# The second map's exponentials kept in their PSUM bank, and the mixing weight taken by one VectorE operation with two scalars

## The chip, the cores and the metric

The kernel runs on one core of a Trainium2 chip. The metric is the device time of one execution in microseconds (us), lower is better. The core's engines each run their own queue of instructions and wait for one another by semaphores: PE (TensorE, matmuls), DVE (VectorE), ACT (ScalarE), POOL (GpSimd) and SP (here only a queue of DMAs).

## What is computed

Two layers of a decoder over 512 tokens of width 1024. Each layer is a SwiGLU feed-forward block, a mixer, and a second feed-forward block, each followed by a layer norm. The mixer has three groups of heads; the change touches the differential attention heads:

```python
s = jnp.einsum('bqhmd,bkhmd->bhmqk', q_blk, k) * scale      # m = 0, 1: two maps per head
s = s - slopes[None, :, None, None, None] * dist[None, None, None]
s = jnp.where(dist >= 0, s, NEG_INF)
p = jax.nn.softmax(s, axis=-1)
a = (p[:, :, 0] - lam * p[:, :, 1]).astype(v.dtype)
return jnp.einsum('bhqk,bkhe->bqhe', a, v)
```

With e0 and e1 the exponentials of the two maps and r0 and r1 their row sums, the kernel forms e0 + w e1 with w = -lam r0 / r1, and divides by r0 at the very end.

## The kernel before, in words

All matmuls of size run in fp32 split into a high and a low part (whi, wlo, xhi, xlo), three matmuls for one product. In each layer the attention is one run of 40 steps G = 0 to 39, in five bodies of 8 steps; bodies 1 and 3 (G 8 to 15 and 24 to 31) are the differential heads, two heads of four 128-row query tiles each, so that the width of a step goes 128, 256, 384, 512 and again. There are 32 differential steps in the program. Each step goes through the engines so:

1. PE `scores(G)`: the scores of map m into bank 2*(G%2)+m (L1092, L1094).
2. DVE `row_max(G)`: L1515. Then ACT `exp(G)`: L777, from the bank into s32, with the row sum into rsum. For a differential step there are two, m = 0 and 1.
3. DVE `mix(G)`: L1530 takes the reciprocals of the two row sums, L1532 the weight wlam (one value per partition), L1536 the mix of the two maps, in place in s32.
4. PE `turn_p(G)`: transposes (L1104) into bank 4+G%2; ACT `p_hi(G)` (L784) and DVE `p_lo(G)` (L1542) split it into a high and a low part; PE `values(G)` (L1116, L1118) multiplies by V; DVE `output(G)` (L1553, L1555).

Each engine's order is written out by hand, one G after the other. DVE does per step: row_max(G), output(G-2), mix(G), p_lo(G-1), and then what the body adds (the splits of queries and keys at L1464 and L1469, parts of the output projection's sums at L1283). PE does per step: scores(G), a piece of other matmuls (`between`: projections of later bodies at L1020, in body 3 the early part of the output projection at L857), values(G-2), turn_p(G-1), another piece.

POOL meanwhile loads the stacks of queries and keys of the next body (L574) and takes low parts of weights (L555, a TENSOR_TENSOR over SBUF of 1024 columns), and between its last two stack loads it scales the norm's gain and bias rows (L481, two such operations). The second-to-last stack load waits for the scores of G = 27, the middle of body 3.

The banks 1 and 3 of the second map are used by nothing else in the attention until `turn_y` takes them in body 4.

Of the kernel before, what the change touches and what calls it, by code (L numbers as in the profile page):

```python
# [5 lines left out]
ALU = mybir.AluOpType  # L6
ACT = mybir.ActivationFunctionType
# [14 lines left out]
FOX_P, DIFF_P = FOX_H // 2, DIFF_H // 2  # L22
# [35 lines left out]
STEPS = 2 * NT  # L58
# [29 lines left out]
def build(nc, x_in, a_w, b_w, d_w, gb_row, gb_col, mix_row, mix_col, ws_in, lamv, out):  # L88
    ctx = ExitStack()
    with ctx:  # L90
# [8 lines left out]
        bank = [ctx.enter_context(nc.psum_tensor(f"bank{i}", [P, 512], F32)) for i in range(8)]  # L99
# [10 lines left out]
        s32 = sb("s32", [P, 4, 512])  # L110
# [39 lines left out]
        negm = sb("negm", [P, 4])  # L150
        olo = sb("olo", [P, 2, HD])
        rsum = sb("rsum", [P, 4])
        rinv = sb("rinv", [P, STEPS, 2])
        wlam = sb("wlam", [P, STEPS])
# [6 lines left out]
        nlam1 = sb("nlam1", [P, 1])  # L161
# [86 lines left out]
        exp_ok = [sem(f"exp_ok{m}") for m in range(2)]  # L248
        rinv_ok = sem("rinv_ok")
        wlam_ok = sem("wlam_ok")  # L250
        mixp_ok = sem("mixp_ok")
# [51 lines left out]
        def count(l, G, m):  # L303

            if m == 0:
                return l * ALL + G + 1
            return l * DIFF_P * STEPS + sum(is_diff(g) for g in range(G + 1))
# [322 lines left out]
        def _(act):  # L630
            a = nc.scalar
# [76 lines left out]
            for l in range(L):  # L708
# [60 lines left out]
                def exp(G):  # L769
                    for m in range(2 if is_diff(G) else 1):  # L770
                        act.wait_ge(max_ok[m], count(l, G, m))
                        if G >= 2:

                            act.wait_ge(pt_done, l * ALL + G - 1)
                        w = (G % NT + 1) * P
                        i = 2 * (G % 2) + m
                        a.activation(s32[:, i, 0:w], bank[i][:, 0:w], ACT.Exp, bias=negm[:, i:i + 1],  # L777
                                     accum_out=rsum[:, i:i + 1]).then_inc(exp_ok[m], 1)

                def p_hi(G):  # L780
# [66 lines left out]
        def _(pe):  # L847
# [178 lines left out]
            def turn_y(l, i):  # L1026

                c = (EARLY + LATE)[i][0]
                if i < len(EARLY):
                    b = 6 + i % 2  # L1030
                else:
                    b = 1 + 2 * (i % 2)
                    if i < len(EARLY) + 2:
                        pe.wait_ge(exp_ok[1], (l + 1) * DIFF_P * STEPS)
                if i % len(EARLY) >= 2:

                    pe.wait_ge(yt_ok, l * NC + i - 1)
                if c < FOX_P:
                    pe.wait_ge(o_ok, l * ALL + (PAIRS.index(c) + 1) * STEPS + AHEAD)
                elif c < FOX_P + DIFF_P:  # L1040
                    pe.wait_ge(y_ok, l * DIFF_P + c - FOX_P + 1 + AHEAD)
                for t in range(NT):
                    ins = t_.transpose(bank[b][:, t * P:t * P + P], nat[:, t, c * P:c * P + P], ident[:, :])
                ins.then_inc(yt_done, 1)
# [31 lines left out]
            def heads(l):  # L1076

                def scores(G):
                    b, k = divmod(G, STEPS)
                    hh, t = divmod(k, NT)  # L1080
                    n_ = (t + 1) * P
                    tile = stack[hh]
                    if t == 0:
                        pe.wait_ge(stacked[hh], 32 * (l * BODIES + b + 1))
                    maps = 2 if is_diff(G) else 1
                    for m in range(maps):
                        i = 2 * (G % 2) + m
                        if G >= 2 and count(l, G - 2, m) > 0:

                            pe.wait_ge(exp_ok[m], count(l, G - 2, m))  # L1090
                        for n in (range(2) if maps == 1 else (m,)):
                            t_.matmul(bank[i][:, 0:n_], tile[0:STACK, n, t * P:t * P + P], tile[0:STACK, 2 + n, 0:n_],  # L1092
                                      start=(n == 0 or maps == 2), stop=False)
                        t_.matmul(bank[i][:, t * P:n_], identr[:, :], maskr[:, :], start=False, stop=True).then_inc(s_done[m], 1)  # L1094

                def turn_p(G):
                    if is_diff(G):
                        pe.wait_ge(mixp_ok, count(l, G, 1))
                    else:
                        pe.wait_ge(exp_ok[0], count(l, G, 0))  # L1100

                    pe.wait_ge(o_ok, l * ALL + max(G - 1, 0) + AHEAD)
                    for e in range(G % NT + 1):
                        ins = t_.transpose(bank[4 + G % 2][:, e * P:e * P + P], s32[:, 2 * (G % 2), e * P:e * P + P], ident[:, :])  # L1104
                    ins.then_inc(pt_done, 1)

                def values(G):
                    b, k = divmod(G, STEPS)
                    hh, t = divmod(k, NT)

                    pe.wait_ge(pt_ok, l * ALL + G + 1)
                    vc = PAIRS[b] * 2 * HD + hh * HD

                    both = bank[4 + G % 2][:, 0:2 * HD].rearrange("p (a n) -> p a n", a=2)
                    for e in range(t + 1):
                        t_.matmul(both, pthi[G % 2][:, e * P:e * P + P], vals[:, e, :, vc:vc + HD],  # L1116
                                  start=(e == 0), stop=(e == t), skip_group_check=True)
                        ins = t_.matmul(both[:, 0, :], ptlo[G % 2][:, e * P:e * P + P], vhi[:, e, vc:vc + HD],  # L1118
                                        start=False, stop=(e == t), skip_group_check=True)
                    ins.then_inc(pv_done, 1)  # L1120

                for G in range(ALL):
                    b, k = divmod(G, STEPS)
                    if k == 0 and b <= EARLY_BODY:
                        between = early(l) if b == EARLY_BODY else project(l, b + 2)
                    scores(G)
                    next(between, None)
                    if G >= 2:
                        values(G - 2)
                    if G >= 1:  # L1130
                        turn_p(G - 1)
                    next(between, None)
                    if b == BODIES - 1 and k in LATE_TURNS:
                        turn_y(l, LATE_TURNS[k])
                early_output(l, 6, 2)
                values(ALL - 2)
                early_output(l, 6, 3)
                turn_p(ALL - 1)
                early_output(l, 7, 2)
                early_output(l, 7, 3)  # L1140
                late_weights(l, 0)
                for o in range(2):
                    late_output(l, o, 0)
                values(ALL - 1)
                for o in range(2, 4):
                    late_output(l, o, 0)
                late_weights(l, 1)
                for o in range(2):
                    late_output(l, o, 1)
                turn_y(l, NC - 1)  # L1150
                for o in range(2, 4):
                    late_output(l, o, 1)
                for n in range(2, len(LATE)):
                    late_weights(l, n)
                    for o in range(4):
                        late_output(l, o, n)
                for o in range(4, 8 - HELD):
                    for n in range(len(LATE)):
                        late_output(l, o, n)
# [82 lines left out]
        def _(dve):  # L1242
            v = nc.vector
# [151 lines left out]
            for l in range(L):  # L1395
# [8 lines left out]
                def values(j):  # L1404

                    lo, at, n_ = V_PARTS[j]
                    for t in range(NT):
                        src = bank[t + 4 * (j % 2)]
                        dve.wait_ge(vhi_ok, l * 3 * NT + j * NT + t + 1)
                        if j == 0:  # L1410
# [7 lines left out]
                                       op0=ALU.mult, op1=ALU.min).then_inc(fneg_ok, 1)  # L1418
# [105 lines left out]
                def mix(G):  # L1524

                    i = 2 * (G % 2)
                    j = G % STEPS
                    dve.wait_ge(exp_ok[0], count(l, G, 0))
                    dve.wait_ge(exp_ok[1], count(l, G, 1))
                    v.reciprocal(rinv[:, j, :], rsum[:, i:i + 2]).then_inc(rinv_ok, 1)  # L1530
                    dve.wait_ge(rinv_ok, l * ALL + G + 1)
                    v.scalar_tensor_tensor(out=wlam[:, j:j + 1], in0=rinv[:, j, 1:2], scalar=rsum[:, i:i + 1],  # L1532
                                           in1=nlam1[:, :], op0=ALU.mult, op1=ALU.mult).then_inc(wlam_ok, 1)
                    dve.wait_ge(wlam_ok, count(l, G, 1))
                    w_ = (G % NT + 1) * P
                    v.scalar_tensor_tensor(out=s32[:, i, 0:w_], in0=s32[:, i + 1, 0:w_], scalar=wlam[:, j:j + 1],  # L1536
                                           in1=s32[:, i, 0:w_], op0=ALU.mult, op1=ALU.add).then_inc(mixp_ok, 1)

                def p_lo(G):
# [143 lines left out]
```

## Time and profile before

| | us |
|---|---|
| median of 3 runs | 2052.26 (2048.38 to 2054.08) |
| profiled execution, its own time | 2058.27 |
| its span | 2056.5 |
| PE busy | 1950.1 (95%) |
| DVE busy | 1112.6 (54%) |
| ACT busy | 703.3 (34%) |
| POOL busy | 327.9 (16%) |
| attention of layer 0, about | 488 to 640 in the span |
| attention of layer 1, about | 1500 to 1650 in the span |

The span is the time from the first to the last instruction on the core. An engine's busy time is a sum over stages with different limits, so 95% for PE does not say what a stage waits for: inside the attention that has to be read from the stage itself. PEclk is the clock that TensorE was granted, as a share of 2.4 GHz; 0.50 is 1.2 GHz. DVE, ACT and POOL rows give the duration of an instruction including any time that it was held after its start.

### The profile page before, as it was taken

The numbers are of one execution on the slowest core, as the hardware profiler recorded it, in microseconds if no ns is written. First come the engines' busy times: TensorE is split into PE (matmuls) and PEld (weight loads), VectorE is DVE, ScalarE is ACT, GpSimd is POOL, SyncE is SP. The second block draws the span as 40 slices with busy tenths as digits, with TensorE's granted clock in tenths as the row PEclk, the third lists the DMA queues.
The fourth block names the chain that finished last, engine by engine and source line by source line (L and its number), as shares of the span: only waits on it lengthen the run. The fifth ranks groups of instructions, "written<-read, shape, count | busy, mean of one in ns | idle before, by whom it ended". The sixth has DMA issues, their size and how long they took to land.

```text
span 2056.5 us, 25255 instructions
## 1 busy us (share of the span) xinstructions
PE 1950.1 (95%) x9341; PEld 1632.3 (79%) x9341; DVE 1112.6 (54%) x1792; ACT 703.3 (34%) x1017; POOL 327.9 (16%) x291
## 2 busy tenths in 40 slices
PE   7999999997989999999999999999978899999996
PEld 6888888886777888888788888888867788888885
DVE  6444445562776653444584444546647765444446
ACT  4323322343434433333242222224335343233321
POOL 6000000333314400000150000003332252000002
PEclk9999999998979999999999999999989999999998
DMA  5223233226731323222322223231277132322221
GB/s 219 102 82 107 78 120 110 80 85 176 190 88 62 116 71 119 102 82 102 113 97 88 102 82 120 74 132 70 78 204 193 42 108 78 121 98 86 102 102 41
DMA packets 41922, 216.99 MB, mean 106 GB/s; under 512 B 8724, under 2 KB 9172, under 8 KB 17928
## 3 DMA queue, kind: packets, MB, share of 16 engines
q1 hardware_dynamic: 38984, 200.35, 27.9%
q0 software_dynamic: 2880, 15.90, 3.1%
q8 instruction: 33, 0.54, 0.1%
q14 instruction: 25, 0.20, 0.0%
HBM read 198.28 MB, written 17.93 MB: 105 GB/s over the span
## 4 chain that ended last, share of the span: by engine, by line
PE 80%; DVE 10%; issue 3%; DMA 2%; ACT 2%; SPq 2%; POOL 1%; DVEq 0%; ACTq 0%; POOLq 0%
PE bank L857 74%; PE bank L1020 2%; SPq L391 2%; DVE res L1283 1%; DVE nat L1431 1%; DMA whiD<-stacks 1%; DMA rawA<-in_a_w 1%; PE bank L1116 1%; PE bank L885 1%; DVE st L1307 1%; DVE hl L1358 1%; DVE hl L1542 1%; DVE wlam L1532 1%; PE bank L1104 1%; DVE negm L1515 1%
## 5 line engine op out<-in xcount | busy, mean ns | idle before, releaser
L857 PE MATMUL bank<-whiD,hl 128*128 128x512 f32 x1408 | 444.6, 390 | 5.6 <-DVE hl L1358 5.1
L1283 DVE SCALAR_TENSOR_TENSOR res<-bank,res 128x512 f32<-128x512 f32 x384 | 258.5, 688 | 171.0 <-PE bank L857 168.8
L857 PEld LDWEIGHTS bank<-whiD,hl 128*128 128x128 f32 x1408 | 264.3, 188 | 65.0 <-DVE hl L1358 8.1
L857 PE MATMUL bank<-xhi,whiA 128*128 128x512 f32 (+1 forms) x768 | 287.6, 374 | 10.3 <-DVE xlo L1262 10.3
L857 PE MATMUL bank<-xlo,whiA 128*128 128x512 f32 (+1 forms) x768 | 285.9, 372 | 0.0
L857 PE MATMUL bank<-xhi,wloA 128*128 128x512 f32 (+1 forms) x768 | 285.9, 372 | 0.0
L857 PE MATMUL bank<-wloD,hl 128*128 128x512 f32 x704 | 274.1, 389 | 0.0
L857 PE MATMUL bank<-xhi,whiB 128*128 128x512 f32 x704 | 273.9, 389 | 0.0
L857 PE MATMUL bank<-xlo,whiB 128*128 128x512 f32 x704 | 273.9, 389 | 0.0
L857 PE MATMUL bank<-xhi,wloB 128*128 128x512 f32 x704 | 273.9, 389 | 0.0
L857 PEld LDWEIGHTS bank<-xhi,whiA 128*128 128x128 f32 x768 | 145.5, 189 | 38.0 <-DVE xlo L1262 8.5
L1354 DVE TENSOR_TENSOR s<-s,bank 128x256 f32<-128x256 f32 x88 | 33.1, 418 | 246.7 <-ACT s L690 246.7
L857 PEld LDWEIGHTS bank<-xlo,whiA 128*128 128x128 f32 x768 | 145.5, 189 | 24.9
L857 PEld LDWEIGHTS bank<-xhi,wloA 128*128 128x128 f32 x768 | 145.4, 189 | 25.0
L1251 DVE TENSOR_TENSOR wloA<-rawA,whiA 128x2048 fp32r<-128x2048 f32 x51 | 123.1, 2414 | 74.0 <-ACT whiA L636 74.0
L1347 DVE TENSOR_TENSOR s<-s,bank 128x512 f32<-128x512 f32 x44 | 30.2, 687 | 242.8 <-ACT s L683 242.8
L481 POOL TENSOR_TENSOR gbr<-gbr,alpha 128x1024 f32<-128x1024 f32 x12 | 23.2, 1957 | 862.5 <-DMA gbr<-in_gb_row 862.5
L857 PEld LDWEIGHTS bank<-xhi,wloB 128*128 128x128 f32 x704 | 132.2, 188 | 27.5
L857 PEld LDWEIGHTS bank<-xhi,whiB 128*128 128x128 f32 x704 | 132.2, 188 | 27.3
L857 PEld LDWEIGHTS bank<-xlo,whiB 128*128 128x128 f32 x704 | 132.2, 188 | 27.2
L857 PEld LDWEIGHTS bank<-wloD,hl 128*128 128x128 f32 x704 | 132.2, 188 | 26.9
L690 ACT ACTIVATE s<-bank 128x256 f32<-128x256 f32 x88 | 29.0, 381 | 348.7 <-PE bank L857 348.7
(177 smaller groups left out, 3146.8 us busy)
## 6 DMA issues: line engine op xcount, KB each, us to landing
rawA<-in_a_w SPq DMA_DIRECT2D x63, 1024.0 KB, 4.8
rawB<-in_b_w SPq DMA_DIRECT2D x54, 1024.0 KB, 4.8
rawD<-in_d_w SPq DMA_DIRECT2D x46, 1024.0 KB, 4.8
stacks<-hl SPq DMA_DIRECT2D x240, 64.0 KB, 1.7
whiD<-stacks POOLq DMA_DIRECT2D x10, 768.0 KB, 6.0
wloD<-stacks POOLq DMA_DIRECT2D x10, 768.0 KB, 6.0
gbr<-in_gb_row SPq DMA_DIRECT2D x7, 1024.0 KB, 6.4
out<-nat SPq DMA_DIRECT2D x4, 512.0 KB, 2.6
```

Source lines behind the costliest of these rows:

```text
L391: sp.dma_start(stacks[b, s // 2, j * ROWS:(j + 1) * ROWS, tile + s % 2, :], part[s * ROWS:(s + 1) * ROWS, :].bitcast(F32)).then_inc(put_ok ...
L481: g.tensor_tensor(gbr[:, w, :], gbr[:, w, :], alpha[:, :].broadcast_to([P, D]), ALU.mult).then_inc(rs_step, 1)
L690: a.activation(silu["B"][:, h * 256:h * 256 + 256], bank[2][:, h * 256:h * 256 + 256], ACT.Silu).then_inc(silu_ok["B"], 1)
L857: ins = t_.matmul(out_, a_, b_, start=(start and k == 1), stop=(stop and k == n), skip_group_check=check)
L885: ins = t_.transpose(bank[b][:, lo:lo + P], nat[:, 2 * h + t, c * P:c * P + P], ident[:, :])
L1020: ins = t_.matmul(bank[6 + g][:, :], a_, b_, start=(k == 1), stop=(k == 3 * NC))
L1104: ins = t_.transpose(bank[4 + G % 2][:, e * P:e * P + P], s32[:, 2 * (G % 2), e * P:e * P + P], ident[:, :])
L1116: t_.matmul(both, pthi[G % 2][:, e * P:e * P + P], vals[:, e, :, vc:vc + HD], start=(e == 0), stop=(e == t), skip_group_check=True)
L1251: v.tensor_tensor(wlo[s][:, :], raw[s][:, :], f32(whi[s][:, :]), ALU.subtract).then_inc(lo_ok[s], 1)
L1283: v.scalar_tensor_tensor(out=r, in0=bank[b][:, :], scalar=scale, in1=r, op0=ALU.mult, op1=ALU.add).then_inc(step, 1)
L1347: v.tensor_tensor(h32["A"], silu["A"], bank[1][:, :], ALU.mult).then_inc(h32_ok["A"], 1)
L1354: v.tensor_tensor(h32["B"][:, t], silu["B"][:, t], bank[3][:, t], ALU.mult).then_inc(h32_ok["B"], 1)
```

## The change

Three things. ACT's exponentials of the second map (m = 1) are written back into the bank that they are read from, where they went to s32. The mix reads the second map from that bank. And the weight wlam, before a SCALAR_TENSOR_TENSOR with two tensors (rinv, nlam1) and a scalar (rsum), is a TENSOR_SCALAR with one tensor (rinv) and two scalars (rsum, nlam1). Two waits of PE that guard banks 1 and 3 are set to the mix (mixp_ok) in place of the exponential (exp_ok[1]).

```diff
@@ ACT, exp(G)
-                        a.activation(s32[:, i, 0:w], bank[i][:, 0:w], ACT.Exp, bias=negm[:, i:i + 1],
+                        a.activation(bank[i][:, 0:w] if m else s32[:, i, 0:w], bank[i][:, 0:w], ACT.Exp, bias=negm[:, i:i + 1],
                                      accum_out=rsum[:, i:i + 1]).then_inc(exp_ok[m], 1)
@@ PE, turn_y
                     if i < len(EARLY) + 2:
-                        pe.wait_ge(exp_ok[1], (l + 1) * DIFF_P * STEPS)
+                        pe.wait_ge(mixp_ok, (l + 1) * DIFF_P * STEPS)
@@ PE, scores(G)
-                            pe.wait_ge(exp_ok[m], count(l, G - 2, m))
+                            pe.wait_ge(mixp_ok if m else exp_ok[0], count(l, G - 2, m))
@@ DVE, mix(G)
-                    v.scalar_tensor_tensor(out=wlam[:, j:j + 1], in0=rinv[:, j, 1:2], scalar=rsum[:, i:i + 1],
-                                           in1=nlam1[:, :], op0=ALU.mult, op1=ALU.mult).then_inc(wlam_ok, 1)
+                    v.tensor_scalar(wlam[:, j:j + 1], rinv[:, j, 1:2], rsum[:, i:i + 1], nlam1[:, :],
+                                    ALU.mult, ALU.mult).then_inc(wlam_ok, 1)
...
-                    v.scalar_tensor_tensor(out=s32[:, i, 0:w_], in0=s32[:, i + 1, 0:w_], scalar=wlam[:, j:j + 1],
+                    v.scalar_tensor_tensor(out=s32[:, i, 0:w_], in0=bank[i + 1][:, 0:w_], scalar=wlam[:, j:j + 1],
                                            in1=s32[:, i, 0:w_], op0=ALU.mult, op1=ALU.add).then_inc(mixp_ok, 1)
```

On DVE, at the first differential step of layer 0 (G = 8), the rows around the mix stand so (s is s32, nlam is nlam1, hl holds the low parts):

```order
 L1555 SCALAR_TENSOR_TENSOR nat<-bank,rinv,olo 128x64
 L1530 RECIPROCAL rinv<-rsum 128x2
-L1532 SCALAR_TENSOR_TENSOR wlam<-rinv,rsum,nlam 128x1
-L1536 SCALAR_TENSOR_TENSOR s<-s,wlam 128x128
+L1532 TENSOR_SCALAR wlam<-rinv,rsum,nlam 128x1
+L1536 SCALAR_TENSOR_TENSOR s<-bank,wlam,s 128x128
 L1542 TENSOR_TENSOR hl<-bank,hl 128x512
 L1469 TENSOR_TENSOR hl<-bank,hl 128x512
```

Nothing moves in DVE's order; two of the instructions are of another kind or read another memory, and so it is in all 32 steps.

On PE, at the last step of the first head of body 1 (width 512), the scores of the second map carry another wait:

```order
 L1092 MATMUL bank<-whiD 128x512 [waits exp_ok0]
 L1094 MATMUL bank<-maskr,identr 128x128
-L1092 MATMUL bank<-whiD 128x512 [waits exp_ok1]
+L1092 MATMUL bank<-whiD 128x512 [waits mixp_ok]
 L1094 MATMUL bank<-maskr,identr 128x128
 L1020 MATMUL bank<-xhi,whiA 128x512
```

PE's instructions and their order are unchanged, and POOL's too; only the semaphore of this wait differs.

## Rows read from the trace of the kernel before

**Rows 1.** The profile's page: the span, and the chain that ended last.

```profile
span 2056.5 us, 25255 instructions
...
PE 80%; DVE 10%; issue 3%; DMA 2%; ACT 2%; SPq 2%; POOL 1%; DVEq 0%; ACTq 0%; POOLq 0%
```

**Rows 2.** Stretches of 4 us in body 3: busy time, granted clock.

```profile
core 0: us, PE busy (x) PEld busy (x) DVE busy (x) ACT busy (x) POOL busy (x), PEclk, DMA share, GB/s
...
588.00:592.00 4.00, 1.37 (x8) 0.84 (x7) 3.96 (x2) 0.05 (x1) 3.39 (x2) 1.00 0.80 197
592.00:596.00 4.00, 3.27 (x13) 3.08 (x14) 3.07 (x11) 1.41 (x5) 0.00 (x0) 0.58 0.00 0
```

**Rows 3.** Line L1532: duration in ns, minimum, median, maximum.

```profile
L1532 DVE SCALAR_TENSOR_TENSOR wlam<-rinv,rsum,nlam x32: 219/220/3462, 519.4 to 1618.3; 128x1 f32<-128x1 f32 x32
```

**Rows 4.** Groups of DVE by line and shape: total busy, mean ns.

```profile
L1532 DVE SCALAR_TENSOR_TENSOR wlam<-rinv,rsum,nlam 128x1 f32<-128x1 f32 x32 | 15.4, 482 | 1.2
...
L1536 DVE SCALAR_TENSOR_TENSOR s<-s,wlam 128x512 f32<-128x512 f32 x8 | 6.0, 751 | 0.3
...
L1458 DVE SCALAR_TENSOR_TENSOR nat<-bank,mixc,nat 128x256 f32<-128x256 f32 x12 | 4.9, 477 | 0.1
L1274 DVE TENSOR_SCALAR nat<-res,mv,rstd 128x1024 f32<-128x1024 f32 x6 | 4.9, 811 | 2.2 <-POOL rstd L528 2.2
...
L1536 DVE SCALAR_TENSOR_TENSOR s<-s,wlam 128x256 f32<-128x256 f32 x8 | 3.9, 485 | 0.3
...
L1400 DVE TENSOR_SCALAR mixr<-mixr,olam 128x256 f32<-128x256 f32 x2 | 0.7, 344 | 0.0
```

**Rows 5.** Timeline 521 to 524, body 1 of layer 0: start, duration.

```profile
521.32 2.39 POOL L555 TENSOR_TENSOR wloA<-rawA,whiA 128x1024 fp32r<-128x1024 f32 x1 [5.00 <-ACT whiA L643]
...
522.21 0.28 DVE L1555 SCALAR_TENSOR_TENSOR nat<-bank,rinv,olo 128x64 f32<-128x64 f32 x1
...
522.93 0.81 DVE L1532 SCALAR_TENSOR_TENSOR wlam<-rinv,rsum,nlam 128x1 f32<-128x1 f32 x1
```

**Rows 6.** Timeline 583 to 602, body 3 of layer 0.

```profile
586.58 1.05 POOL L574 DMA_DIRECT2D whiD<-stacks  x2 [10.10 <-PE bank L1094]
...
587.62 3.78 POOL L481 TENSOR_TENSOR gbr<-gbr,alpha 128x1024 f32<-128x1024 f32 x2
...
587.96 3.46 DVE L1532 SCALAR_TENSOR_TENSOR wlam<-rinv,rsum,nlam 128x1 f32<-128x1 f32 x1
...
592.73 0.47 PE L1116 MATMUL bank<-vals,hl 128*128 128x128 f32 x1 [3.36 <-DVE hl L1542]
...
600.85 0.22 DVE L1532 SCALAR_TENSOR_TENSOR wlam<-rinv,rsum,nlam 128x1 f32<-128x1 f32 x1
```

**Rows 7.** DVE timeline 1595 to 1618, body 3 of layer 1.

```profile
1598.85 3.22 DVE L1532 SCALAR_TENSOR_TENSOR wlam<-rinv,rsum,nlam 128x1 f32<-128x1 f32 x1
...
1611.13 0.22 DVE L1532 SCALAR_TENSOR_TENSOR wlam<-rinv,rsum,nlam 128x1 f32<-128x1 f32 x1
```

**Rows 8.** DVE timeline 530 to 538, body 1 of layer 0.

```profile
530.08 0.22 DVE L1532 SCALAR_TENSOR_TENSOR wlam<-rinv,rsum,nlam 128x1 f32<-128x1 f32 x1
...
537.02 0.59 DVE L1532 SCALAR_TENSOR_TENSOR wlam<-rinv,rsum,nlam 128x1 f32<-128x1 f32 x1
```

**Rows 9.** The chain in order of time, 490 to 660: weights, start and length.

```profile
522.93 0.82 DVE wlam L1532
...
587.96 3.47 DVE wlam L1532
```

**Rows 10.** Timelines of POOL and of DVE, 425 to 450, layer 0.

```profile
432.03 9.82 POOL L496 TENSOR_TENSOR res<-res,gbr 128x1024 f32<-128x1024 f32 x4
...
432.11 10.00 DVE L1431 TENSOR_SCALAR nat<-nat,gmv,grs 128x384 f32<-128x384 f32 x4 [1.20 <-POOL grs L518]
```

**Rows 11.** Groups of ACT by line and shape: total busy, mean ns.

```profile
L694 ACT ACTIVATE hl<-s 128x256 fp32r<-128x256 f32 x88 | 33.0, 419 | 9.3 <-DVE s L1354 9.3
L690 ACT ACTIVATE s<-bank 128x256 f32<-128x256 f32 x88 | 29.0, 381 | 348.7 <-PE bank L857 348.7
```

## The prediction

> **What bounds the kernel now.** Read the page first: the chain that ended last lies on PE for 80% and on DVE for 10% [rows 1]. Outside the attention PE is simply fed; the changed instructions all lie inside it, so the windows of that stage come next. In body 3 of layer 0 the stretch from 588 to 592 has PE busy for 1.37 us of 4 while DVE is busy for 3.96 with only two instructions, and in the next stretch TensorE's granted clock is 0.58 where it was 1.00 [rows 2]. So there is a place where one long DVE instruction stops everything.
>
> The line view names it. The weight wlam at L1532 takes 220 ns at the median, one value per partition, and 3462 ns at most [rows 3]. Its 32 executions are busy for 15.4 us [rows 4]; at 220 ns each they would be 7.0, so 8.4 us are time in which a tiny instruction was held. The timeline says by what. In body 1 a POOL operation over SBUF runs from 521.32 for 2.39, to 523.71; the weight starts at 522.93 and ends at 523.74, just behind it [rows 5]. In body 3 the two gain operations of POOL run from 587.62 to 591.40 and the weight, started at 587.96, ends at 591.42 [rows 6]. There are six such long weights in the program, and each ends within 0.03 us of the end of a POOL operation; these two are the first and the third of them. Inside the same POOL operation the STT at L1555, which reads a bank, a scalar and one SBUF tensor, takes 0.28 [rows 5] and isn't held. The weight reads two SBUF tensors (rinv and nlam1), and so does the mix behind it.
>
> Here the Trainium skill bears on the rows (SBUF — State Buffer, section "Who interferes with whom"): a VectorE instruction with two SBUF inputs and a GpSimd instruction that reads SBUF share a port pair as an exclusive lock, and the second waits for the first to end. By that rule the trace agrees for the SCALAR_TENSOR_TENSOR form.
>
> Behind the held weight stand, in DVE's queue, the mix and then p_lo of the step before, for which PE's `values` waits: PE sits idle for 3.36 us until 592.73 [rows 6]. The chain in order of time runs through the held weights [rows 9]. So the 8.4 us are on the path.
>
> **The change part by part.**
>
> *The weight's wait.* If the new form isn't held, the four waits in the two bodies 1 go, and the two long ones in bodies 3. The long ones are 3.46 - 0.22 = 3.24 [rows 6] and 3.22 - 0.22 = 3.00 [rows 7]; the rest of 8.4 is 2.16, in bodies 1. In those the clock is full and nothing else is late: minus 2.16.
>
> In bodies 3 more than the wait hangs on it, since PE's clock falls behind the idle time [rows 2]. I take two steps together, from the weight of G = 27 to that of G = 29: 600.85 - 587.96 = 12.89 in layer 0 [rows 6], 1611.13 - 1598.85 = 12.28 in layer 1 [rows 7]. The same two steps of body 1, at full clock and with no wait in between, take 537.02 - 530.08 = 6.94 [rows 8]. Their work is nearly the same: body 3 has an addition at L1283 that body 1 lacks, body 1 a query split at L1464 of about the same length. So bodies 3 give 5.95 + 5.34 = 11.29 if the clock stays up, and 6.24 if it falls all the same. Body 1 has gaps on PE of its own, and the clock stays; I take 11.29. Sum of this part: -13.45, bounds -8.4 and, if the new form is held as before, 0.
>
> *The weight's own cost.* No row shows a TENSOR_SCALAR with two scalars on one column. With one scalar and 256 columns it takes 344 ns [rows 4]; with two and 1024 columns 811 [rows 4]. The mix gains 751 - 485 = 266 ns over 256 columns, 1.04 a column [rows 4]; 1024 columns in 811 ns leave no room for that, so the TENSOR_SCALAR in SBUF does two columns in the time of one, 0.52 each. That leaves fixed parts of 344 - 133 = 211 and 811 - 533 = 278. So the new weight should take some 280 ns where it took 220: +60 ns, 32 times, all behind ACT's exponential on DVE's path: +1.9 us. Bounds 0 and 1.9.
>
> *The mix.* It reads one operand from a bank. The nearest pair at 256 columns: 485 ns from SBUF twice, 477 from a bank and SBUF at L1458 [rows 4]: -8 ns, 32 times, -0.25.
>
> *The second exponential.* It writes to a bank instead of SBUF, and no row has ACT writing a bank. From reading: 419 ns from SBUF, 381 from a bank at 256 columns [rows 11]. As bounds I take that difference of 38 ns either way, times 32: -1.2 to +1.2, and zero in the sum, since an input's row says little of an output. The Trainium skill (ScalarE: Activation LUTs, section "Step-by-step: what each stage is for") calls PSUM the quicker destination for ScalarE; it gives no figure, and no run here shows it yet.
>
> *The two waits of PE.* scores(G) now wait for the mix of G-2, not its exponential. PE executes turn_p(G-2) one step before scores(G), and turn_p already waits for that same mix, so the semaphore is always there: zero. turn_y in body 4 follows turn_p of G = 31 in the same way: zero. If either did bite, the price would be what lies between exponential and mix, the weight's 0.22 and the widest mix's 0.75, some 1.0 us a step. No DMA and no place in SP's or POOL's queue moves.
>
> What is late next, once the weight is free: DVE itself, as in body 1, where it is never idle for long. A gain there stays, because everything behind (key splits, then SP's puts, the loads, POOL's halves) starts from DVE or PE events that come earlier by the same amount.
>
> Sum: -13.45 + 1.9 - 0.25 = -11.8. The profiled execution took 2058.27, which becomes 2046.5. It lies 6 us above the median of the runs shown; the same 11.8 off the median, 2052.26, gives 2040.5.
>
> **The rivals.**
>
> *The new weight is held all the same.* This is the change not doing what it must. TENSOR_SCALAR from SBUF to SBUF, one tensor and two scalars, is just the kind of L1431, and there four of them with 384 columns take 10.00 us beside POOL's four operations of 9.82 [rows 10]: each is held behind one. The wide form waits; whether the form with a single column does is shown by no row. For its being free speaks that the wide form does two columns at a time, and one column leaves nothing to pair. Then nothing of the 13.45 comes: +1.9 - 0.25, so 2053.9. [...] I call it 0.33.
>
> *The gain is given back.* PE gets through the steps and stands before something that doesn't come earlier, as stacks or weights on their way from memory. The load of body 4's first stack is issued at 586.58 [rows 6], and needed only by the scores of G = 32, three steps after the weight at 600.85 [rows 6], so body 3's part is safe; body 1's part and that of the clock could go, leaving about -6.2 + 1.65 = -4.6: 2047.7. 0.06.
>
> *Slower: the new weight is held by more than before.* If the form is one that also waits for POOL's stack loads, each of these can hold a weight for up to its 1.05 us [rows 6]. Four in a layer fall in differential bodies, eight in all: 8.4 on top of 1.65, which makes 2062.3. It decides from 4.5 us on, so more than half of that must come about. Against it: a weight starts only every 3.5 us, so a load of 1 us mostly falls between two. 0.04.
>
> **How the numbers follow.** The forecast, the weight free and the waits gone, has 0.57. Its own range: at best the weight costs nothing more and the exponential gains, -13.45 - 0.25 - 1.2, 2037; at worst the clock falls as before, -8.4 + 1.65 + 1.2 = -5.6, 2046.7. I predict 2040.5. The range to hold 8 in 10 must take in the rival that the weight is held, up to 2053.9 + 1.2, so 2036 to 2055. A measurement of this kernel tells about 0.3% from no change, here 6.2 us, so below 2046.1 is faster: 0.57, nearly all of the forecast's cases and a little of the second rival. Within it: 0.38, slower 0.05.
>
> **What would show each step.** Right: L1532 has a maximum near its median, at about 280 ns, and no long one while POOL's gain operations run beside it; the two steps behind G = 27 take about 7 us; the granted clock stays 1.00 there; the mix of 256 columns is near 477 ns. Wrong: L1532 keeps a maximum near 3.4 us that ends with POOL's operation. The clock's share is wrong if the waits are gone and the two steps still take 9 us or more. The exponentials' part shows in L777, map 0 beside map 1, at equal width. The forecast fails most easily on the first of these, on whether one column of a TENSOR_SCALAR waits for POOL.

## The result, and the profile after

The changed kernel takes 2042.02 us at the median of 5 runs (2040.96 to 2045.71), beside 2052.26 for the kernel before: a ratio of 0.9948, 95% interval 0.9933 to 0.9963. Run twice more beside the experiments it gave 0.9955 (0.9941 to 0.9969) and 0.9945 (0.9929 to 0.9960). That is 10 us less; the forecast was 2040.5, 11.8 less.

The page of the profiled execution, whose own time was 2042.62, answers to [rows 1]:

```profile
span 2040.9 us, 25255 instructions
...
PE 82%; DVE 10%; issue 3%; ACT 2%; DMA 2%; SPq 1%; POOL 1%; DVEq 0%; ACTq 0%; POOLq 0%
```

The line view of the weight (minimum, median and maximum in ns) answers to [rows 3]:

```profile
L1532 DVE TENSOR_SCALAR wlam<-rinv,rsum,nlam x32: 272/273/276, 520.1 to 1602.6; 128x1 f32<-128x1 f32 x32
```

The long weights are gone, all 32 of them, and the price is 273 ns where it was 220. In body 3 of layer 0 the timeline of all engines now reads so, where [rows 6] had a weight of 3.46:

```profile
584.70 3.78 POOL L481 TENSOR_TENSOR gbr<-gbr,alpha 128x1024 f32<-128x1024 f32 x2
...
585.28 0.27 DVE L1532 TENSOR_SCALAR wlam<-rinv,rsum,nlam 128x1 f32<-128x1 f32 x1
585.59 0.75 DVE L1536 SCALAR_TENSOR_TENSOR s<-bank,wlam,s 128x512 f32<-128x512 f32 x1
...
591.88 0.27 DVE L1532 TENSOR_SCALAR wlam<-rinv,rsum,nlam 128x1 f32<-128x1 f32 x1
```

POOL's two gain operations start earlier than the weight and last as long as before, and neither the weight nor the mix waits for them. From the weight of G = 27 to that of G = 29 it is 591.88 - 585.28 = 6.60 us; it was 12.89. The windows of this stretch (busy time per engine, then granted clock) answer to [rows 2]:

```profile
584.00:588.00 4.00, 3.59 (x26) 2.98 (x25) 3.51 (x11) 1.72 (x8) 4.00 (x4) 1.00 0.69 162
588.00:592.00 4.00, 4.00 (x25) 3.28 (x24) 3.13 (x12) 2.17 (x9) 0.48 (x1) 1.00 0.19 37
592.00:596.00 4.00, 3.77 (x21) 2.94 (x20) 3.47 (x11) 1.51 (x5) 0.42 (x1) 1.00 0.00 0
```

The weight of G = 27 starts 2.68 us earlier in this execution, so its stretch is the first of the three. PE is busy for 3.59 to 4.00 of 4 us where it had 1.37, and the granted clock stays at 1.00 (2.4 GHz) where it had fallen to 0.58. Another fall of the clock stays: in the three stretches from 572 to 584 it is 0.50 throughout before, and 0.54, 0.50 and 0.68 after. It lies ahead of the weight of G = 27, and the change doesn't touch it. In layer 1 the same two steps, DVE timeline:

```profile
1588.68 0.27 DVE L1532 TENSOR_SCALAR wlam<-rinv,rsum,nlam 128x1 f32<-128x1 f32 x1
...
1595.29 0.27 DVE L1532 TENSOR_SCALAR wlam<-rinv,rsum,nlam 128x1 f32<-128x1 f32 x1
```

That is 6.61 against 12.28. The groups of DVE and of ACT by shape (mean ns behind the comma) give the prices of the other two parts:

```profile
L1536 DVE SCALAR_TENSOR_TENSOR s<-bank,wlam,s 128x512 f32<-128x512 f32 x8 | 6.0, 751 | 0.3
...
L1536 DVE SCALAR_TENSOR_TENSOR s<-bank,wlam,s 128x256 f32<-128x256 f32 x8 | 3.9, 484 | 0.3
```

```profile
L777 ACT ACTIVATE s<-bank,negm 128x256 f32<-128x256 f32 x20 | 9.5, 474 | 14.8 <-DVE negm L1515 14.8
...
L777 ACT ACTIVATION_READ_ACCUMULATOR bank<-bank,negm 128x1 f32 x32 | 6.4, 199 | 0.0
...
L777 ACT ACTIVATE bank<-bank,negm 128x256 f32<-128x256 f32 x8 | 3.5, 438 | 0.0
```

The mix costs what it did (751, 484 against 751, 485). An exponential written to its bank takes 36 ns less than one written to SBUF, and the read of its row sum 6 ns more (199 against 193).

### The profile page after: what moved, and what is told of

Read it like the earlier page. It is cut to its first block, busy times and chain, and to the rows that moved or that the text cites. A ratio compares the mean times of both kernels' runs of the same rounds, so it can differ in the third digit from the quotient of the medians.

```text
span 2040.9 us, 25255 instructions
## 1 busy us (share of the span) xinstructions
PE 1940.7 (95%) x9341; PEld 1624.7 (80%) x9341; DVE 1102.0 (54%) x1792; ACT 702.7 (34%) x1017; POOL 327.7 (16%) x291
## 4 chain that ended last, share of the span: by engine, by line
PE 82%; DVE 10%; issue 3%; ACT 2%; DMA 2%; SPq 1%; POOL 1%; DVEq 0%; ACTq 0%; POOLq 0%
PE bank L857 74%; PE bank L1020 3%; DVE res L1283 1%; DMA whiD<-stacks 1%; SPq L391 1%; PE bank L1116 1%; DVE nat L1431 1%; PE bank L885 1%; DVE st L1307 1%; PE bank L1104 1%; DVE hl L1542 1%; DVE negm L1515 1%; PE bank L1092 1%; PE bank L1118 1%; DVE hl L1358 1%
```

## The experiments

The theory: POOL's operations over SBUF hold a DVE instruction that reads two SBUF tensors; so both the weight and the mix had to lose one of theirs, and the fallen clock hangs on the stop that the hold makes. The rivals: one of the two parts was enough; a TENSOR_SCALAR is free whatever its width; the clock fell for a reason of its own. A hold is the time by which an instruction lasts longer than its like elsewhere, while POOL works. Times are medians. The kernel before, run beside each on the same chip, had 2053.45 beside the weight alone, the bank alone, two columns and the later gain; 2052.95 beside three columns, the stop and the first try at a better version; 2050.70 beside the second try.

**The weight alone.** Before, with this edit only:

```diff
-                    v.scalar_tensor_tensor(out=wlam[:, j:j + 1], in0=rinv[:, j, 1:2], scalar=rsum[:, i:i + 1],
-                                           in1=nlam1[:, :], op0=ALU.mult, op1=ALU.mult).then_inc(wlam_ok, 1)
+                    v.tensor_scalar(wlam[:, j:j + 1], rinv[:, j, 1:2], rsum[:, i:i + 1], nlam1[:, :],
+                                    ALU.mult, ALU.mult).then_inc(wlam_ok, 1)
```

> Before, with the weight alone as TENSOR_SCALAR; exponentials and mix stay in SBUF, so the mix still reads two SBUF tensors. Theory (whatever reads two SBUF tensors is held by POOL): the weight takes 273 ns always, the mix behind it takes up the hold, its 512-wide form up to about 3.9 us; time 2052 to 2055, no gain. Rival (only the weight's form matters): the mix stays at 751 ns at most, time 2041 to 2044.

Measured: 2052.62, ratio 0.9995 (0.9987 to 1.0004), no change clear of the noise. The timeline of all engines in body 3 of layer 0 shows where the hold went:

```profile
584.98 3.77 POOL L481 TENSOR_TENSOR gbr<-gbr,alpha 128x1024 f32<-128x1024 f32 x2
...
585.86 0.27 DVE L1532 TENSOR_SCALAR wlam<-rinv,rsum,nlam 128x1 f32<-128x1 f32 x1
...
586.17 3.15 DVE L1536 SCALAR_TENSOR_TENSOR s<-s,wlam 128x512 f32<-128x512 f32 x1
```

The weight slips through beside POOL, and the mix, still on two SBUF tensors, takes 3.15 for its 0.75: it is held until POOL's second operation is over at 588.75. Over all steps the mixes of 512 and of 256 columns have means of 1411 and 571 ns where they had 751 and 485 [rows 4], eight of each, so 6.0 us of holds where the weights had 8.4. So the rival that the weight was enough falls. The interval still allows this half of the change 2.7 us on its own.

**The bank alone.** After, with the weight as it was:

```diff
-                    v.tensor_scalar(wlam[:, j:j + 1], rinv[:, j, 1:2], rsum[:, i:i + 1], nlam1[:, :],
-                                    ALU.mult, ALU.mult).then_inc(wlam_ok, 1)
+                    v.scalar_tensor_tensor(out=wlam[:, j:j + 1], in0=rinv[:, j, 1:2], scalar=rsum[:, i:i + 1],
+                                           in1=nlam1[:, :], op0=ALU.mult, op1=ALU.mult).then_inc(wlam_ok, 1)
```

> After, with the weight again a SCALAR_TENSOR_TENSOR on two SBUF tensors; exponentials and mix in the bank. Theory: the weight is held as before, up to 3.4 us, and the only gain is that of the exponentials, 32 times 37 ns = 1.2 us: 2050 to 2052. Rival (the bank is what brought the gain): 2042 to 2044.

Measured: 2054.20, ratio 1.0005 (0.9997 to 1.0014). Its line view:

```profile
L1532 DVE SCALAR_TENSOR_TENSOR wlam<-rinv,rsum,nlam x32: 219/220/3280, 519.8 to 1615.6; 128x1 f32<-128x1 f32 x32
```

The weight is held as before. The 1.2 us that I expected of the exponentials don't show; the interval allows 0.6 at most. So neither half gains anything clear of the noise without the other, and together they gain 10 us.

**The weight over two columns, and over three.** After, with the weight's operation over the pair of reciprocals. Only the second result is used. wlam has a column for each result; for three columns rinv is one column wider, too, the third being filled once with ones.

```diff
-                    v.tensor_scalar(wlam[:, j:j + 1], rinv[:, j, 1:2], rsum[:, i:i + 1], nlam1[:, :],
+                    v.tensor_scalar(wlam[:, j, :], rinv[:, j, :], rsum[:, i:i + 1], nlam1[:, :],
                                     ALU.mult, ALU.mult).then_inc(wlam_ok, 1)
...
-                    v.scalar_tensor_tensor(out=s32[:, i, 0:w_], in0=bank[i + 1][:, 0:w_], scalar=wlam[:, j:j + 1],
+                    v.scalar_tensor_tensor(out=s32[:, i, 0:w_], in0=bank[i + 1][:, 0:w_], scalar=wlam[:, j, 1:2],
```

> After, with the weight's TENSOR_SCALAR over two columns of rinv instead of one (the first column's result is not used). Theory that the form is free only because one column has nothing to pair: with two columns it is held as the wide ones of L1431 are, up to 3.4 us, and the time goes back to 2050 to 2053. Rival (a narrow TENSOR_SCALAR, or one whose scalars are both per partition, is never held): at most 280 ns, time 2041 to 2043.

> After, with the weight's TENSOR_SCALAR over three columns (odd, the same count in source and destination; only one result is used). If a form is held when its columns can be split between two ports, and an odd equal count can, then it is held, up to 3.4 us. If only an even count is held, it takes 272 to 280 ns at most.

Measured: 2054.46, ratio 1.0004 (0.9995 to 1.0013), for two columns; a single run of 2054.46 for three. The line view of the one with two:

```profile
L1532 DVE TENSOR_SCALAR wlam<-rinv,rsum,nlam x32: 286/289/3493, 517.8 to 1616.1; 128x2 f32<-128x2 f32 x32
```

and of the one with three:

```profile
L1533 DVE TENSOR_SCALAR wlam<-rinv,rsum,nlam x32: 286/289/3233, 518.9 to 1614.4; 128x3 f32<-128x3 f32 x32
```

One column more brings the whole hold back, and with it the whole loss. With two columns the long weight of layer 0 starts at 585.68, takes 3.49 and ends at 589.17, and POOL's second gain operation ends at 589.15. Two and three columns are held, one is not. The rival of the prediction was thus right about the instruction and wrong only about its smallest form. The Trainium skill (Vector Engine (DVE) Microarchitecture Reference, section 5.1) gives a TENSOR_SCALAR in SBUF a mode on both read ports if its most major dimension of more than one element is even, or odd and of the same size in source and destination. The holds at two and at three columns agree with it. A single column has no such dimension; the page doesn't say what it does, and here none of 32 was held.

**POOL's gain operations later.** Before, with this edit to POOL's order:

```diff
                 load_stack(BODIES - 1, 0)
-                scale_gain(3 * l + 2)
                 load_stack(BODIES - 1, 1)
+                scale_gain(3 * l + 2)
```

> Before, with POOL's two gain operations moved behind the last stack load, out of body 3. The two long holds of the weight (3.24 and 3.00 us) go, the four short ones of bodies 1 stay. If the fallen clock belongs to the hold, the two steps behind G = 27 take 7 us instead of 12.9 and 12.3, and 11.3 us are gained: 2041 to 2042. If the clock falls all the same, 6.2 us: 2046.

Measured: 2048.00, ratio 0.9972 (0.9964 to 0.9981): 5.5 us less, half of the first expectation. The two steps behind G = 27 take 6.51 us now in both layers (in layer 0 the weights start at 585.84 and 592.35), at full clock. But the timelines of POOL and of DVE show that the operations met the last weight of body 3:

```profile
597.06 3.76 POOL L481 TENSOR_TENSOR gbr<-gbr,alpha 128x1024 f32<-128x1024 f32 x2
...
599.52 1.33 DVE L1532 SCALAR_TENSOR_TENSOR wlam<-rinv,rsum,nlam 128x1 f32<-128x1 f32 x1
```

and the windows that PE ran dry behind it and its clock fell:

```profile
600.00:604.00 4.00, 1.85 (x13) 1.71 (x14) 3.42 (x7) 0.93 (x3) 0.81 (x1) 0.95 0.25 51
604.00:608.00 4.00, 4.00 (x19) 3.57 (x18) 1.49 (x5) 0.88 (x4) 0.00 (x0) 0.62 0.02 4
```

Behind a hold of 1.1 us in place of 3.2 stands the same kind of fall 12 us later. The weight that it holds is the last one of body 3, so the run's whole time is no clean measure, but body 3 up to there is one: from its first weight to its last it is 36.25 and 34.84 us before (layers 0 and 1), 29.05 and 29.08 here, and 29.27 and 29.33 in the changed kernel. With the old weight and the old mix, and only POOL's operations out of the way, body 3 gets all of its gain. The loss comes behind it: from that last weight of layer 0 to the first weight of layer 1 it is 927.1 us against 923.8 to 924.6 in three traces of the changed kernel, and from the last weight of layer 1 to the end 441.0 against 438.3. Each hold of 1.1 us so costs some 3 us here.

**A stop without POOL.** After, with DVE stopped behind the weight of G = 27 by fillings of an idle tile (each waits for the one before):

```diff
+                    if G == 3 * STEPS + NT - 1:
+                        for n in range(6):
+                            v.memset(sq[:, :, 0:122], 0.0).then_inc(stop_ok, 1)
+                            dve.wait_ge(stop_ok, l * 6 + n + 1)
```

> After, with six fillings of the idle tile sq, about 0.56 us each, put on DVE behind the weight of G = 27 in each layer: DVE stops for some 3.4 us without POOL having any part. If the stop itself makes TensorE's clock fall, the two steps from G = 27 to G = 29 take about 12 us and the kernel loses 3.4 + 2 to 2.5 us per layer, 11 to 12 in all: about 2053.5. If the clock fell for another reason, only the stops are lost, 6.8 us: about 2049.

Measured: 2053.51, ratio to before 1.0003 (0.9994 to 1.0012), beside 2041.98 for the changed kernel: 11.5 us lost. The DVE timeline:

```profile
588.14 0.27 DVE L1533 TENSOR_SCALAR wlam<-rinv,rsum,nlam 128x1 f32<-128x1 f32 x1
588.46 0.47 DVE L1537 MEMSET sq<- 128x488 f32 x1
...
592.13 0.75 DVE L1541 SCALAR_TENSOR_TENSOR s<-bank,wlam,s 128x512 f32<-128x512 f32 x1
...
600.64 0.27 DVE L1533 TENSOR_SCALAR wlam<-rinv,rsum,nlam 128x1 f32<-128x1 f32 x1
```

and the windows:

```profile
588.00:592.00 4.00, 1.32 (x8) 0.82 (x6) 3.07 (x8) 0.21 (x1) 3.34 (x2) 0.99 0.87 197
592.00:596.00 4.00, 2.60 (x11) 2.54 (x12) 3.27 (x11) 0.96 (x5) 0.00 (x0) 0.50 0.00 0
```

The mix starts 3.99 us behind the weight where it was 0.31, a stop of 3.68 in each layer, 7.4 in all. The time lost is 4 us more than that. The two steps take 12.50 where they took 6.60, and 13.39 where they took 6.61 in layer 1: 5.9 and 6.8 for a stop of 3.7. The clock falls to 0.50 behind the stop, and a 512-column matmul of L858 takes 0.63 us there where its like takes 0.40 at full clock. POOL's gain operations run beside the stop, as they do in the changed kernel, where the clock stays up; the fillings take their 0.47 each beside them and are not held. This is the picture of [rows 2], made by hand.

**A better version, in two tries.** POOL's weight half in body 2 also holds the last norm stage of the first differential pair, L1507, whose multiplication reads nat and mixr, two SBUF tensors: its longest took 1.71 us in the changed kernel for some 0.28. First for both pairs:

```diff
-                    if b - 1 in DIFF_AT and 2 <= k <= 5:
-                        rms(DIFF_AT.index(b - 1), k - 2)
+                    if b - 1 in DIFF_AT and k in (2, 3, 4, 6):
+                        rms(DIFF_AT.index(b - 1), min(k - 2, 3))
```

> After, with the last norm stage of the first differential pair (L1507, reads two SBUF tensors, held about 1.5 us by POOL's weight half in body 2) moved from step 5 to step 6 of its body. If it is no longer held, 1.5 us per layer on a stretch where DVE is the bound, so 3 us: 2039; and if that stretch is what makes TensorE's clock fall at the start of body 3, up to 5 us more. If the hold is hidden, no change.

Measured: 2053.22, ratio 1.0000 (0.9991 to 1.0009): all of the change's gain lost, 11.2 us. The timeline of all engines in body 4 of layer 0:

```profile
617.59 5.22 DVE L1507 TENSOR_TENSOR nat<-nat,mixr 128x128 f32<-128x128 f32 x4
617.82 4.84 POOL L555 TENSOR_TENSOR wloD<-rawD,whiD 128x1024 fp32r<-128x1024 f32 x2 [5.34 <-PE bank L1094]
...
622.96 1.08 PE L1043 MATMUL bank<-ident,nat 128*128 128x128 f32 x4 [3.04 <-DVE nat L1507]
```

and the window behind it:

```profile
624.00:628.00 4.00, 4.00 (x14) 2.86 (x13) 1.82 (x5) 1.09 (x4) 0.00 (x0) 0.50 0.65 258
```

For the second pair the later place meets two of POOL's weight halves, PE's transposes wait 3.04 for it, and the clock, which is 1.00 there in the changed kernel, falls to 0.50. The first pair did gain: from the last weight of body 1 to the first of body 3 it is 24.45 and 24.54 us (layers 0 and 1) where the changed kernel has 25.87 and 25.86. So for the first pair alone:

```diff
-                    if b - 1 in DIFF_AT and 2 <= k <= 5:
-                        rms(DIFF_AT.index(b - 1), k - 2)
+                    if b - 1 == DIFF_AT[0] and k in (2, 3, 4, 6):
+                        rms(0, min(k - 2, 3))
+                    if b - 1 == DIFF_AT[1] and 2 <= k <= 5:
+                        rms(1, k - 2)
```

> After, with the last norm stage (L1507) moved from step 5 to step 6 for the first differential pair alone; for the second it stays at step 5, since at step 6 it meets POOL's halves of the output weights and PE's transposes wait for it. The hold of 1.5 us per layer in body 2 goes and no new one comes: 2039 against 2042 for the changed kernel. If the loss of the run before had another cause than the second pair, it stays near 2053.

> The changed kernel a third time, beside the one above on the same chip: 2041 to 2043.

Measured: 2037.49, ratio to before 0.9935 (0.9918 to 0.9952), beside 2040.68 and 0.9945 for the changed kernel. Its line view has no held one left:

```profile
L1507 DVE TENSOR_TENSOR nat<-nat,mixr x16: 283/286/293, 559.9 to 1614.8; 128x128 f32<-128x128 f32 x16
```

The median is 3.2 us lower, as expected, while the two intervals overlap. The traces show the gain in its place: from the last weight of body 1 to the first of body 3 it is 24.45 and 24.60 us, where three traces of the changed kernel have 25.86 to 26.64, so at least 1.2 us a layer. The clock still falls at the start of body 3 (0.50 from 572 to 576), so the 5 us more of the expectation before stay away. The changed kernel had run beside the stop and the first try, too, and took 2041.98 there:

> The changed kernel once more, beside the others on one chip: 2041 to 2043.

## Why the prediction was right

**The weight's wait.** The step that everything hung on, whether one column of a TENSOR_SCALAR waits for POOL, came out as forecast, with a chance of 0.57 that the rows could not raise: no row of the trace had it, and the two- and three-column forms show how near the rival was. That it came out free was in part luck. Its reason, nothing to pair in one column, agrees with all three widths; other reasons that treat one column alone would agree as well.

**What hung on it.** The two steps of body 3 were to take 6.94 and took 6.60 and 6.61, so this term was 11.96 us between the two profiles where I had 11.29. The clock's share in it is real: the stop made by hand cost 4 us more than its length. Each stop of 3.7 had 5.9 and 6.8 as its price in its layer's two steps, the held weights of 3.24 and 3.00 had 6.29 and 5.67.

**The weight's own cost.** 273 ns against 280 forecast, so +1.7 us for 1.9.

**The mix.** -8 ns forecast, 1 found (484 for 485): the term of -0.25 was nothing. L1458, from which it came, has another pattern of columns, and its 7 ns less did not carry over.

**The second exponential.** Zero in the sum; it is -36 ns, near the bound of -38, with 6 back for its row sum, so -1.0 us over 32 steps. The run with the bank alone shows none of it in the time.

**PE's two waits.** No effect is seen, as forecast: in the changed kernel PE's waits between 515 and 625 are for p_lo (8.3 us), the key split (2.2) and an output's low part (0.9), and none is for the mix.

**The sum.** -11.8 forecast, -10.2 at the median of the first comparison and -10.0 to -11.0 in the later ones. The 95% interval of the first comparison, 7.6 to 13.8 us, holds both the forecast and the measured value, so what is missing of it can't be put down to a term. Between the two profiled executions it is 15.6, more than my terms give. The traces say where 2.7 of it lie: from the last weight of body 1 to that of G = 27 in layer 0, before took 44.00 us and after 41.28, but the run with the bank alone, whose weight is held as before, took 41.34. The clock had fallen earlier in before: it is 0.59 from 568 to 572, where after has 1.00. So this part is how one execution differs from another, not the change, and it was right to take the sum as a difference off the median. Why the clock falls earlier in one execution than in another stays open.

## What to carry to other kernels

Look for a tiny vector instruction with a large maximum: its end beside the end of a GpSimd operation names the cause. Then mend every instruction behind it that reads two SBUF tensors, or is a TENSOR_SCALAR in SBUF over more than one column; here, mending the first alone handed the hold to the next. And when an operation is moved out of the way, look up what it meets at its new place: of three such moves here, one met a shorter hold and kept half of its gain, one met a longer one and lost more than it gained, and only the third met none.

## What the runs showed of the hardware that was not expected

- A TENSOR_SCALAR with two scalars per partition, in SBUF, waits for GpSimd with two and with three columns (maximum 3.49 and 3.23 us) and never with one (none of 32, 0.276 at most), in the same place of the same program.
- By an estimate, a second scalar per partition, with the second operation that it serves, costs the TENSOR_SCALAR some 60 ns: at 0.52 ns a column the 344 ns of one scalar leave a fixed part of 211 [rows 4], and the whole one-column operation with two takes 273. No run took the scalar away alone.
- The third column cost a TENSOR_SCALAR with two scalars nothing (289 ns at the median with two and with three), the second cost 16 ns (273 with one).
- The held instruction did not get in between two GpSimd operations that stood one behind the other: the weight that started 0.34 us into the first was let go at the end of the second, 3.46 us on [rows 6], while the four TENSOR_SCALARs of L1431 took turns with POOL's four [rows 10].
- ScalarE's exponential in place in a PSUM bank takes 36 ns less than into SBUF at 256 columns (438 against 474), and its accumulator read 6 ns more.
